# A two-layer hybrid decoder trunk: four value tiles at a time written in token form, the S5 products spread over projection tiles, and a constant load put later

## The reference

```
proj = h @ w_in                        # 256 x 2048 by 2048 x 5168
m_qk, m_v, m_o, m_i, m_f, s_u, n_q, n_kv, n_g = split(proj)
y_m = mlstm(m_qk, m_v, m_o, m_i, m_f)  # 4 heads of 128
y_s = s5(s_u)                          # 32 groups, state of 64 complex; scan, gelu, glu
y_n = nsa(rope(n_q), k_cmp, v_cmp, k_slc, v_slc, k_win, v_win, gates)  # 8 heads, 2 kv heads
y   = concat(y_m, y_s, y_n) @ w_out
```

## Time and profile before

| | |
|---|---|
| median of 3 runs | 2420.58 us (2419.27 to 2421.63) |
| profiled execution | 2424.17 us, of which the span of instructions is 2422.3 us |
| PE busy | 2352.5 us, 97% |
| DVE busy | 1860.4 us, 77% |
| ACT busy | 1287.5 us, 53% |
| granted TensorE clock | 0.993 of full speed in the mean |
| chain that ended last | PE 77%, DVE 14%, DMA 5% |

### The profile page before, as it was taken

The page is one execution under the profiler, slowest core; times in us unless marked ns, Lnnn a source line. Parts: engine busy times, 40 slices in busy tenths (PEclk is TensorE's granted clock), DMA queues, the critical chain, the costliest instruction groups (busy, mean ns, idle before and its releaser), DMA issues.

```text
span 2422.3 us, 40088 instructions
## 1 busy us (share of the span) xinstructions
PE 2352.5 (97%) x13932; PEld 2057.1 (85%) x13932; DVE 1860.4 (77%) x2739; ACT 1287.5 (53%) x2164; POOL 227.5 (9%) x384
## 2 busy tenths in 40 slices
PE   6899999999999999999999999999999999999998
PEld 5689988788888888888889999887888888888887
DVE  7989998879999999666679987567896666565555
ACT  5365755555455545444468657655555445554444
POOL 1111111101111111000001130000110000000000
PEclk9999999999999999999999999999999999999999
DMA  9999878859999999687756865447795555556554
GB/s 379 401 392 325 288 280 303 307 191 354 333 349 346 343 343 338 244 290 275 271 210 221 295 240 197 162 182 268 284 331 193 189 190 188 186 189 199 201 192 146
DMA packets 189211, 643.06 MB, mean 265 GB/s; under 512 B 19089, under 2 KB 41809, under 8 KB 183329
## 3 DMA queue, kind: packets, MB, share of 16 engines
q1 hardware_dynamic: 125346, 421.72, 48.0%
q0 software_dynamic: 51264, 205.04, 23.9%
q10 hardware_dynamic: 12480, 14.72, 1.7%
HBM read 626.68 MB, written 14.71 MB: 265 GB/s over the span
## 4 chain that ended last, share of the span: by engine, by line
PE 77%; DVE 14%; DMA 5%; ACT 2%; issue 2%; POOL 0%; ACTq 0%; DVEq 0%; POOLq 0%; SPq 0%
PE ps L1346 25%; PE ps L815 18%; PE ps L1354 13%; PE ps L798 8%; PE ps L1243 4%; DVE w_lo L2015 3%; DVE ada_w L2021 3%; DVE mix L2015 2%; DMA ada_w<-ada_d 2%; PE ps L783 2%; DMA ada_lo<-ada_d 1%; PE ps L1257 1%; ACT w_hi L1427 1%; DVE side L2015 1%; DMA ring<-stream 1%
## 5 line engine op out<-in xcount | busy, mean ns | idle before, releaser
L2015 DVE TENSOR_TENSOR w_lo<-ring,w_hi 128x1024 fp32r<-128x1024 f32 x708 | 868.4, 1232 | 427.3 <-ACT w_hi L1427 423.4
L1427 ACT ACTIVATE w_hi<-ring 128x1024 fp32r<-128x1024 f32 x708 | 748.7, 1058 | 787.1 <-PE ps L815 245.2
L1346 PE MATMUL ps<-hT,w_hi 128*128 128x512 f32 x2688 | 642.2, 391 | 0.0
L1346 PEld LDWEIGHTS ps<-hT,w_hi 128*128 128x128 f32 x2688 | 493.8, 188 | 95.8
L2021 DVE SCALAR_TENSOR_TENSOR ada_w<-ada_w,cs_row 128x1024 f32<-128x1024 f32 (+1 forms) x332 | 406.6, 1258 | 16.2 <-DMA ada_w<-ada_d 15.9
L798 PE MATMUL ps<-hT,w_hi 128*128 128x256 f32 x2176 | 407.5, 289 | 5.0 <-DVE w_lo L2015 2.9
L798 PEld LDWEIGHTS ps<-hT,w_hi 128*128 128x128 f32 x2176 | 343.4, 194 | 15.3 <-issue 12.7
L1354 PEld LDWEIGHTS ps<-hT,w_lo 128*128 128x128 f32 x2688 | 344.6, 191 | 13.1
L1354 PE MATMUL ps<-hT,w_lo 128*128 128x256 f32 x2688 | 348.7, 283 | 0.0
L798 PE MATMUL ps<-hT,w_lo 128*128 128x256 f32 x1088 | 309.7, 285 | 0.0
L798 PEld LDWEIGHTS ps<-hT,w_lo 128*128 128x128 f32 x1088 | 210.6, 194 | 0.0
(11 more groups left out here) (327 smaller groups left out, 2361.2 us busy)
## 6 DMA issues: line engine op xcount, KB each, us to landing
ring<-stream SPq DMA_DIRECT2D x746, 512.0 KB, 4.8
ada_w<-ada_d POOLq DMA_DIRECT2D x320, 512.0 KB, 6.5
ada_w<-ada_d POOLq DMA_DIRECT2D x12, 1024.0 KB, 12.4
ada_lo<-ada_d POOLq DMA_DIRECT2D x10, 1024.0 KB, 15.5
ada_hi<-ada_d POOLq DMA_DIRECT2D x10, 1024.0 KB, 11.9
mix<-stream SPq DMA_DIRECT2D x14, 512.0 KB, 14.5
xs<-x SPq DMA_DIRECT2D x2, 2048.0 KB, 11.1
s_in_w<-mix ACTq DMA_DIRECT2D x8, 512.0 KB, 6.7
```

Of the source, the lines that this page charges most:

```text
L1346: m = pe.matmul(ps[:, bank, :], w_hi[:, (c + half) % SPLIT, kk * P:(kk + 1) * P], hT[:, k, :, :], start=k == 0, stop=k == KT - 1)
L1427: s.activation(w_hi[:, c % SPLIT, :], ring[:, at % RING, :], ACT.Copy).then_inc(hi_ready, 1)
L2015: return v.tensor_tensor(o, a, b, op)
```

## The change

**Token form.** `ORDER` becomes U, KC, VC, KS, KW, then VS and VW (tiles 12 to 15), the gates (16), Q, QK, then V (tiles 33 to 36), O. The two groups of four value tiles (`TOK`) are no longer computed as channels by tokens. A new `tok_proj` keeps h as the stationary operand and streams the weights of all four tiles, 4 x 128 columns, through it: 24 matmuls of 512 columns for each quarter of the group, 96 in all. Two PSUM banks, one for each half of the tokens, collect over all four steps, and ACT copies each of them out once (`tok_out`). `v_tokens` and `m_tokens` go, with their signals.

**Loads.** The chunks of these tiles are cut across four tiles of the stream, in contiguous pieces of 1 KB instead of 4 KB; for VS and VW each chunk is two DMAs.

**S5 products.** One S5 product is issued after each three matmuls of a tile's half, eight to a half: `s5_in` in tiles 18, 19 (second halves) and 21 (both halves), `s5_out` in the second halves of tiles 22 to 27, one `s5_out` to a tile. The gelu of the second half is thereby at tile 27.

**Constants.** 670 KB of constants, on POOL's queue before behind row 5 of the head's 32 rows of the adaLN matrix, are issued behind the last of them.

**DVE.** In layer 0 the late `s5_weights_c` comes before the rope of the same step, and the first three ropes one step earlier.

```diff
-ORDER = (*range(T_U, T_Q), *range(T_KV, T_QK), GATES, *range(T_Q, T_KV), *range(T_QK, NPROJ), *range(T_U))
+TOK = ((T_VS, T_VS + 1, T_VW, T_VW + 1), (T_V, T_V + 1, T_V + 2, T_V + 3))
+ORDER = (*range(T_U, T_Q), *range(T_KV, T_VS), T_KW, T_KW + 1, *TOK[0], GATES, *range(T_Q, T_KV), *range(T_QK, T_V), *TOK[1],
+         *range(T_U))
...
-OUT_AT = [OUT_TILE + i for i in (0, 1, 2, 3, 4, 4)]
+OUT_AT = [OUT_TILE + i for i in range(6)]
+IN_HALF = ((IN_TILE, 1), (IN_TILE + 1, 1), (IN_TILE + 3, 0), (IN_TILE + 3, 1))
...
-                if n == HEAD_SLOTS - 1:
-                    pool.dma_start(cst[:, K_FIRST:], consts[:, K_FIRST:]).then_inc(cst_rest, 16)
+            pool.dma_start(cst[:, K_FIRST:], consts[:, K_FIRST:]).then_inc(cst_rest, 16)
...
+                        if beside:
+                            beside(half, kk)
...
+            def tok_proj(l, n):
+
+                i, j = tok_slot(n)
+                ends = j in (0, NTOK - 1)
+                older = N_TOK[i] % 2
+                tiles = (older, 1 - older) if j == 0 else (0, 1)
+                steps = [(h, t) for t in tiles for h in range(2)] if ends else [(h, t) for h in range(2) for t in tiles]
+                for at, (half, t) in enumerate(steps):
+                    c = 2 * n + half
+                    if t == tiles[0]:
+                        split_ready(l * NS + c)
+                    elif j == 0 and half == 0:
+                        tile_free(l, n - 1)
+                    w = [x[:, c % SPLIT, :].rearrange("p (c k n) -> p c k n", c=4, k=2) for x in (w_hi, w_lo)]
+                    ts_ = slice(t * P, (t + 1) * P)
+                    for kk in range(2):
+                        k = 4 * j + 2 * half + kk
+                        for p, (h, ww) in enumerate(((hT_hi, 0), (hT_hi, 1), (hT_lo, 0))):
+                            m = pe.matmul(ps[:, t, :], h[:, k, ts_], w[ww][:, :, kk, :],
+                                          start=k == 0 and p == 0, stop=k == KT - 1 and p == 2)
+                    if t == tiles[1]:
+                        m.then_inc(w_used, 1)
+                    elif j == NTOK - 1 and half == 1:
+                        tok_first.by(m)
...
+                def s5_beside(n, half, j):
+
+                    for i, at in enumerate(IN_HALF):
+                        if at == (n, half):
+                            s5_in(*divmod(i, 2), j)
+                    if half == 1 and n in OUT_AT:
+                        s5_out(*divmod(OUT_AT.index(n), 3), j)
...
-                def v_tokens(a):
...
-                def m_tokens(ck):
...
+                    slot = tok_slot(n)
+                    if slot and slot[1] == NTOK - 1:
+                        tok_out(slot[0], 0)
                     if n or not l:
                         w_head(2 * n + AHEAD)
-                    in_tile(n)
+                    if not slot:
+                        in_tile(n)
+                    elif slot[1] == NTOK - 1:
+                        tok_out(slot[0], 1)
                     w_head(2 * n + AHEAD + 1)
...
-                    if n in (ITEM_TILE - 2, ITEM_TILE):
-                        a = (n - ITEM_TILE + 2) // 2
-                        vt_mm.wait(s, l, a + 1)
-                        s5_h.wait(s, l, 2)
-                        vt_ev.by(s.activation(vtok[:, a, :, :, :].rearrange("p h s e -> p (h s e)"), ps[:, 4, :], ACT.Copy))
...
+                    if l == 0 and k in LATE_C:
+                        s5_weights_c(len(HEAD_OWN) + LATE_C.index(k))
                     if l == 0 and k in ROPE_V:
                         rope(ROPE_V.index(k))
...
-ROPE_V = [HT - 1, HT + 1, HT + 3] + ROPE_AT[2:]
+ROPE_V = [HT - 2, HT, HT + 2] + ROPE_AT[2:]
```

More of the change, by code:

```diff
@@ L560, in _, with fill, load @@
             sp.dma_start(xs[:, :, :], x.rearrange("b (t p) d -> p (b t) d", p=P)).then_inc(x_in, 16)
-            def load(l, at, src):
+            def fill(to, parts, full):
+                w = CH // len(parts)
+                for i, a in enumerate(parts):
+                    sp.dma_start(to[:, i * w:(i + 1) * w].rearrange("p (t n) -> p t n", n=2 * P), a).then_inc(full, 16)
+            def load(l, at, src, tokens=False):
                 s = at % RING
@@ L961, in s5_tokens, with s5_in @@
                     m.then_inc(s5_ut, 1)
-                def s5_in(h, part):
+                def s5_in(h, part, j):
                     n = R_IN + 2 * h + part
-                    raw_full(l, n)
-                    if h == 0 and part == 0:
-                        s5_tr_ev.wait(pe, l, UT)
-                        s5_u.wait(pe, l, 1)
-                    if h == 1:
-                        s5_bv.wait(pe, l, 1)
-                    for j in range(SH):
-                        m = pe.matmul(ps[:, 2 + part, j * SN:(j + 1) * SN], raw(l, n)[:, j * P:(j + 1) * P],
-                                      s5_u2[:, SH * h + j, :], start=True, stop=True)
-                    raw_used.by(m)
@@ L977, in s5_out @@
[L977 to L994 removed]
+                    if j == 0:
+                        raw_full(l, n)
+                        if h == 0 and part == 0:
+                            s5_tr_ev.wait(pe, l, UT)
+                            s5_u.wait(pe, l, 1)
+                        if h == 1:
+                            s5_bv.wait(pe, l, 1)
@@ new lines, in s5_in, with s5_out @@
+                    m = pe.matmul(ps[:, 2 + part, j * SN:(j + 1) * SN], raw(l, n)[:, j * P:(j + 1) * P],
+                                  s5_u2[:, SH * h + j, :], start=True, stop=True)
+                    if j == SH - 1:
+                        raw_used.by(m)
+                def s5_out(h, part, j):
+                    n = R_OUT + 3 * h + part
+                    if j == 0:
+                        raw_full(l, n)
+                        if part == 1:
+                            s5_h.wait(pe, l, h + 1)
+                        if h == 0 and part == 0:
+                            ch_g.wait(pe, l, 2)
+                    js = slice(j * P, (j + 1) * P)
+                    if part == 0:
+                        m = pe.matmul(ps[:, 6 - h, j * SN:(j + 1) * SN], raw(l, n)[:, js], s5_u2[:, SH * h + j, :],
+                                      start=j == 0, stop=False)
+                    else:
+                        m = pe.matmul(ps[:, 6 - h, j * SN + 1:(j + 1) * SN], raw(l, n)[:, js],
+                                      s5_v[h][part - 1][:, j * SN:(j + 1) * SN - 1], start=False,
+                                      stop=part == 2 and j == SH - 1)
+                    if j == SH - 1:
+                        raw_used.by(m)
```

149 lines of the change are left out of this document (70 added, 79 removed).

## The result

| | before | changed |
|---|---|---|
| median | 2420.39 us (6 runs) | 2438.48 us (6 runs) |
| lowest to highest | 2418.60 to 2421.63 | 2431.43 to 2443.59 |
| profiled execution, its span | 2424.17, 2422.3 | 2431.43, 2429.6 |
| PE busy | 2352.5 us | 2342.0 us |

The ratio is 1.0075, 95% interval 1.0058 to 1.0092: the change makes the kernel slower by 14 to 22 us. The forecast was +2.2 us (2422.8) with a range of 2411 to 2430. A second set of five runs of the same code gave 2435.19 us (2430.92 to 2435.96), ratio 1.0058 (1.0045 to 1.0071). So the traces show 7.3 us of a loss of 15 to 18 (medians), and the rest shows only in the times.

What follows compares the result with a forecast made beforehand. PE bounds layer 1 (nearly always busy), DVE the layer 0 stretch from 283 to 404 us. Head -0.8, layer 0 +3.0 and layer 1 0.0 sum to +2.2 us: 2422.8 us median, called no change, range 2411 to 2430.

Steps and rivals of the forecast that it cites:

- gelu in front of the exps, with its clock, both layers: Gelu behind tile 27 delays first exps: PE waits +3.9 in layer 1, low clock +1.2, layer 0 +3.0 us.
- token form, transposes, head, DVE's order: Layer 1 savings: VS and VW 1.3, V 1.6, transposes 1.7 us; head with constants and DVE's order -0.8 us.
- spreading, and raw chunks wanted earlier: S5 products spread within tiles: -0.5 us in layer 1, 0 in layer 0; earlier wanted raw chunks not priced separately.
- The main term: Gelu behind tile 27 delays the first exps; PE waits 3.9 us before layer 1's second scores, DVE at layer 0's weighted(0).
- savings of 5.4 us: Booked gains: 1.3 for VS and VW, 1.6 for V, 1.7 for transposes in layer 1, 0.8 in the head.
- The 1.2 for the low clock: Layer 1, behind PE's wait for the exps: lower granted clock slows matmuls by 1.7 us, of which 1.2 was taken.
- Its price in layer 0: DVE waits 3.9 us at weighted(0) for the delayed exps, wins back 0.9 at later DMA waits: +3.0 us.
- The waits inside tiles: Layer 0: raw chunk wanted 2.9 us earlier cuts tile 26 by about 4 us; tile 27 still ends near 282.
- the slower rival: Raw chunk waits inside layer 0 tiles 24, 26 and layer 1 tiles 20 to 21, low clock: +8.3 us, 2429; chance 0.31.
- Token form in layer 1: VS and VW tiles 12 to 15 save 1.3 us, V tiles 33 to 36 1.6, transposes 1.7.
- The head: Start of kernel: constants moved back bring the last adaLN row 1.6 us earlier; with DVE's order and 1 KB pieces, -0.8 us.
- the faster rival: Spread hides S5 weight loads, 3.5 us less in layer 1, and layer 0's stall is short: -7.7 us, 2413; chance 0.27.

Runs made afterwards that it cites:

- e12: Kernel before with only the second half's gelu moved behind tile 27, S5 products still in pieces: 2429.56 us, ratio 1.0038.
- e2: Changed kernel with S5 products again in pieces behind tiles 18 to 26 and the second gelu back behind tile 26: 2421.06 us, ratio 1.0008.
- e8: Kernel before with only the S5 products spread as in the changed kernel, so the second gelu is behind tile 27: 2434.45 us, ratio 1.0059.
- e14: Kernel before with S5 products spread mostly over the half tile behind their old place, second gelu behind tile 27: 2429.81 us, ratio 1.0045.
- e1: Changed kernel with the first exps issued in front of the second S5 gelu at tile 27: 2433.28 us, ratio 1.0047.
- e3: Changed kernel with the 670 KB of constants back behind row 5: 2432.18 us, ratio 1.0051.
- e4: Changed kernel with the last two s5_out in both halves of tile 26 and the second gelu behind tile 26: 2432.51 us, ratio 1.0058.
- e5: Changed kernel with token-tile chunks read in 4 KB pieces, one DMA each (wrong weights, all else the same): 2431.46 us, ratio 1.0054.
- e13: Kernel before with S5 products spread, the last two s5_out in both halves of tile 26, second gelu behind tile 26: 2438.14 us, ratio 1.0071.
- e6: Changed kernel with S5 in pieces, second gelu behind tile 26, constants back behind row 5: 2421.60 us, ratio 1.0004.
- e10: Changed kernel with S5 in pieces, constants early, DVE's old order, and 4 KB pieces in one DMA each (wrong weights): 2418.88 us, ratio 0.9997.
- e7: Changed kernel with S5 in pieces, constants early and DVE's order as before, leaving token form with its loads: 2419.78 us, ratio 0.9995.
- e9: Changed kernel with each raw chunk of s5_in and s5_out one place earlier in SyncE's order: 2441.09 us, ratio 1.0080.

## Why the prediction was wrong

Beside the terms of the sum, what the runs give for them, each against before on its own chip:

| term | forecast, us | shown, us | from |
|---|---|---|---|
| gelu in front of the exps, with its clock, both layers | +3.9 + 1.2 + 3.0 | +8.8 | e12 alone |
| token form, transposes, head, DVE's order | -1.3 - 1.6 - 1.7 - 0.8 | +1.2 (-0.2 to +3.9) | e2 |
| spreading, and raw chunks wanted earlier | -0.5 and nothing | +5 | e8 less e12 or e14 |
| sum | +2.2 | +15 | changed kernel: 14.5 and 18.1 |

The main term held. Two steps failed: the raw chunks wanted half a tile earlier were priced at nothing, and savings of 5.4 us were counted of which the time shows none.

- **The gelu in front of the exps** was read rightly off ACT's order and its rows: 3.9 us forecast for layer 1, 3.67 measured in the trace, with +5.0 at the start of tile 28 and +8.95 at that of tile 29. The mechanism holds with nothing else changed (e12), and its whole price, 8.1 us forecast for both layers, was 8.8 there. The 1.2 for the low clock is a mean of two cases: nothing in one trace of the changed kernel, 2.7 us in the other.
- **Its price in layer 0** was +3.0 (a wait of 3.9, 0.9 won back). DVE waited 4.2 us, and the trace has +5.4 between tiles 28 and 30; but 3.5 of it come back by the start of layer 1, where the traces without the moved gelu gain 1.3 to 2.9. From tile 12 of layer 0 to tile 2 of layer 1 both traces of the changed kernel add 3.0 or 3.1 us. So this term was near, though that sum also holds the waits inside tiles. The reason given for winning time back was partly misread: of the 12.6 us of DVE's idle time between 283 and 404 us, 5.0 are waits on DMAs.
- **The waits inside tiles** are the first step that failed. The prediction saw the raw chunk for tile 26, wrote "So tile 26 is cut by a wait of about 4 us", and put its price at nothing beyond tile 27's end. The same argument, that a chunk is wanted 2.9 us earlier while its slot comes free by DVE's pace, holds for each S5 group but the third `s5_in`, which stands half a tile later than before. It cut tiles 18, 22 and 24 of layer 0, and not tile 26, to which PE came late enough by then; in the traces 8 to 12 us more than at tile 12 are gone by the end of tile 24 (in e1, e3, e4, e5, e8 and both of the changed kernel), of which some 7 come back by tile 28 (4 in e4). This was the slower rival, with 0.31 and 2429 us; it named tile 24, was the right case and still 6 to 10 us short, and its sign, a wait over 1 us inside tile 26, did not come. Moving the gelu back in the presence of the waits left the ratio at 1.0058 (e4), and early wants without the gelu cost 17 us where they were wanted earlier still (e13).
- **Token form in layer 1**, in the second step that failed: -4.6 forecast for three terms, about -2.7 in the traces of e6 and e10 (2.0 in e7, which has another wait of 0.6). V gave 4 x 0.27 = 1.1 us for 1.6; I had taken 5.85 us as a tile's time where the tiles concerned take 5.75. VS and VW gave nothing for 1.3, since PE was not the chain at the first of them (e6, above). The transposes gave 1.6 for 1.7. None of it is seen in the times.
- **The head**, in the same step: -0.8 forecast, +1.8 in both traces of the changed kernel. The last row of the adaLN matrix was no longer the last thing waited for. I had the lead of four chunks as the cover for the 1 KB pieces; at the end of the head there is no lead, because SP's queue was still full of earlier loads. The head's own last chunks (KS and KW) are two DMAs each as well in the changed kernel, which the prediction didn't count. The Trainium skill's figure of 512 bytes ("DMA: Bandwidth & Descriptors", section "Specifications"), by which the pieces are free, is neither shown wrong nor right here: doubled loads and constants moved at the same time, and e10 against e7 is 0.9 us, inside the interval.
- **Not visible in a trace.** The medians lie 4 to 7 us above the profiled executions of the changed kernel, whose times spread over 12 us in six runs and over 5 in the five of the second set, against 3 in six of before (8 in the 17 of the next set). What the recorded times add is the mean granted clock: in the six runs it is 0.994 at 2431.43 us and 0.987 at 2443.59, in the five of the second set 0.988 to 0.993 without that order. Long executions of two other kernels are profiled, e1 at 2439.47 and e7 at 2424.80, each the longest of its runs: in both a `ring<-stream` load of the head took 25 to 27 us to land, the last adaLN row landed 3 to 5 us late, and tile 12 starts at +4.6 and +5.0. In e1 tile 24 ends at +16.7 and layer 1 begins at +12.7. So single late loads in the head can make a part of the spread. Whether the long executions of the changed kernel itself are like this was not seen: its two profiles are of 2431.43 and 2431.51 us. The cause of the 7 to 11 us that its traces lack stays open.
- **S5's products** cost 0.22 us each, spread or not, against a saving of 3.5 us a layer for the faster rival (whose sum also has 1.9 for V where the forecast has 1.6, without a source). What the Trainium skill says of loads under a running matmul ("TensorE: Matmul & The Clock Gate", "Part 2: What happens when you issue a matmul") does not show as a saving for 64-column fp32 products between 256-column ones here.

## What to carry to other kernels

When a step is moved earlier on one engine, list for every operand it reads which hand frees its buffer, and price each arrival, not only the last. Where an order is kept by a ring with one spare slot, work that wants its chunk half a tile earlier either waits or takes the slot of the main stream (e8, e9). A wait of 4 us on PE between projection tiles cost 4 to 7 us, by whether the clock fell behind it. A long block of work on ACT delayed whichever `exps` stood behind it, the first or the second (e1, e12). A saving on PE is to be booked only at tiles where PE is the chain, one by one: here the first of eight token tiles in layer 1 was not.

No version here beats both kernels clearly. The token form with its loads alone, S5 in pieces, is at 0.9995 (0.9987 to 1.0004) of before.

## What the runs showed of the hardware

- PE's idle time can cost more than itself: behind 4.1 us of wait the granted clock was 0.68 and tile 29 took 6.76 instead of 5.84 us (e12). Behind the wait of 3.67 us at the same place it was 1.00 in one trace of the changed kernel, with tile 29 at 5.84, and 0.50 in the other. So it is not the length of the wait alone.
- Three DVE instructions of 128x640 took 1.80 us each beside a rope on POOL and 0.83 without it (e6 and before, layer 1 near tile 12).
- A profiled execution can lie on either side of the median: +3.8 us before, -7.1 changed. The runs' mean granted clock, 0.987 to 0.994 in the first six of the changed kernel, was lowest in the longest.
- SP's issue of ten 256 KB loads in 1 KB pieces stretched over 21 us, that of five 512 KB loads in 4 KB pieces, the same bytes, over 17.5 us; both contain waits for the slots, so the share of the pieces in it is not shown.
